# First weight piece in two parts, and the last norm's sums and updates regrouped, in a two-block kernel

## The reference

```python
def rmsnorm(x, g):
    xf = x.astype(jnp.float32)
    var = jnp.mean(xf * xf, axis=-1, keepdims=True)
    return (xf * lax.rsqrt(var + RMS_EPS) * g.astype(jnp.float32)).astype(x.dtype)
...
        h = rmsnorm(h_res, g_mix_pre[l])
        proj = h @ w_in[l]
...
        u_gate, u_val = jnp.split(u, 2, axis=-1)
        f = jax.nn.gelu(u_gate, approximate=True) * u_val
        y = f @ w_down[layer].astype(f.dtype)
        x = x + rms_norm(y, norm_ffn_post[layer])
```

## Time and profile before

| | us |
|---|---|
| median of 3 runs | 1638.5 |
| lowest and highest | 1637.44, 1638.98 |
| the profiled execution | 1639.61 |
| its span | 1637.8 |
| TensorE busy | 1594.1 (97% of the span) |
| VectorE busy | 1112.9 (68%) |
| ScalarE busy | 573.7 (35%) |
| mean granted TensorE clock | 0.991 of full |

### The profile page before, as it was taken

The page is one execution under the profiler, slowest core; times in us unless marked ns, Lnnn a source line. Parts: engine busy times, 40 slices in busy tenths (PEclk is TensorE's granted clock), DMA queues, the critical chain, the costliest instruction groups (busy, mean ns, idle before and its releaser), DMA issues.

```text
span 1637.8 us, 25145 instructions
## 1 busy us (share of the span) xinstructions
PE 1594.1 (97%) x9750; PEld 1431.9 (87%) x9750; DVE 1112.9 (68%) x1624; ACT 573.7 (35%) x826; POOL 32.7 (2%) x65
## 2 busy tenths in 40 slices
PE   8999999989999999999999999999999899999997
PEld 8999999989999988988887888877789788888887
DVE  5334556689888842288899998765557898887324
ACT  5123323442222222253334345556235322222221
POOL 1110000000000000000001101000000000000000
PEclk9999999999999999999999999999999999999999
DMA  4442212222222233233222222222221323232332
GB/s 169 115 128 90 92 63 90 65 91 89 92 90 90 90 103 103 78 110 98 95 90 85 78 84 86 87 67 89 91 91 65 100 93 102 90 102 90 103 113 81
DMA packets 45065, 152.65 MB, mean 93 GB/s; under 512 B 5978, under 2 KB 8038, under 8 KB 44992
## 3 DMA queue, kind: packets, MB, share of 16 engines
q1 hardware_dynamic: 42912, 147.26, 28.1%
q0 software_dynamic: 2080, 4.34, 1.1%
HBM read 149.44 MB, written 4.51 MB: 94 GB/s over the span
## 4 chain that ended last, share of the span: by engine, by line
PE 80%; DVE 15%; ACT 3%; issue 1%; DMA 0%; SPq 0%; DVEq 0%
PE ps L488 70%; PE ps L498 7%; DVE work L1637 6%; DVE wlo L1289 3%; DVE res L1357 1%; DVE tmp L1354 1%; ACT whi L899 1%; PE ps L782 1%; PE ps L851 1%; PE ps L704 1%; ACT probs L1160 1%; ACT L1217 0%; DVE xl L1327 0%; DVE peaks L1681 0%; PE ps L743 0%
## 5 line engine op out<-in xcount | busy, mean ns | idle before, releaser
L488 PE MATMUL ps<-xh,whi 128*128 128x258 f32 (+2 forms) x1944 | 548.2, 331 | 17.6 <-DVE wlo L1289 12.3
L488 PE MATMUL ps<-xh,wlo 128*128 128x258 f32 (+2 forms) x1944 | 541.0, 327 | 0.0
L488 PE MATMUL ps<-xl,whi 128*128 128x258 f32 (+2 forms) x1944 | 540.3, 327 | 0.0
L899 ACT ACTIVATE whi<-raw 128x1024 fp32r<-128x1024 f32 x272 | 287.1, 1057 | 452.0 <-DMA raw<-w_dram 451.6
L1289 DVE TENSOR_TENSOR wlo<-raw,whi 128x1024 fp32r<-128x1024 f32 x272 | 331.7, 1220 | 166.4 <-ACT whi L899 166.0
L488 PEld LDWEIGHTS ps<-xh,whi 128*128 128x128 f32 x1944 | 330.0, 191 | 48.7 <-issue 14.6
L488 PEld LDWEIGHTS ps<-xh,wlo 128*128 128x128 f32 x1944 | 328.6, 190 | 31.6
L488 PEld LDWEIGHTS ps<-xl,whi 128*128 128x128 f32 x1944 | 329.7, 190 | 29.3 <-issue 0.2
L1637 DVE SCALAR_TENSOR_TENSOR work<-cin,vecs,work 128x512 f32<-128x512 f32 x240 | 180.2, 751 | 6.9
L488 PE MATMUL ps<-fh,whi 128*128 128x512 f32 x264 | 103.0, 390 | 1.6 <-DVE stage L1398 0.8
L488 PE MATMUL ps<-fl,whi 128*128 128x512 f32 x264 | 102.8, 389 | 0.0
(11 more groups left out here) (228 smaller groups left out, 2072.5 us busy)
## 6 DMA issues: line engine op xcount, KB each, us to landing
raw<-w_dram SPq DMA_DIRECT2D x272, 512.0 KB, 3.5
bias_copies_dram<-bias_rows_dram POOLq DMA_DIRECT2D x12, 192.0 KB, 3.7
res<-x_dram SPq DMA_DIRECT2D x8, 264.0 KB, 6.3
out_dram<-res SPq DMA_DIRECT2D x16, 128.0 KB, 1.8
dftp<-dftp_dram POOLq DMA_DIRECT2D x1, 550.7 KB, 4.5
bias<-bias_copies_dram POOLq DMA_DIRECT2D x4, 128.0 KB, 2.5
bias<-bias_copies_dram POOLq DMA_DIRECT2D x8, 64.0 KB, 2.6
vecs<-vec_dram SPq DMA_DIRECT2D x1, 364.0 KB, 8.1
```

Of the source, the lines that this page charges most:

```text
L488: last = pe.matmul(ps[:, bank, 0:b - a], w[:, slot, cols], xx[:, k, a:b], start=start and n == 0, stop=stop and n == 2)
L899: act.activation(whi[:, slot, :], raw[:, slot, :], ACT.Copy).then_inc(w_hi, 1)
```

## The change

1. The first piece of weights is loaded in two transfers, columns 0 to 255 (128 KB, the weights of k = 0 and 1 of the first tile) before x's tile 1 and columns 256 to 1023 (384 KB) after it. ScalarE and VectorE split each part by itself. TensorE waits for `first_split` before k = 0 of the first tile and for the whole piece before its k = 2. (The wait on `tile_read` that is removed there concerned a phase with T0 = 0, where it was never made.)
2. In the last norm, at step 21 of the second half, TensorE sums `acc` (which by then holds the squares of tiles 0 to 6) over the channels into one column of PSUM banks 0 and 1 and leaves the sum open; after the last product it adds the squares of tile 7 from `sq` itself. ScalarE's root reads the two columns. VectorE's `add_half` of tile 7 is gone.
3. The last products `down` are made for two k at a time, four instructions of 2 x 256 columns, with the factor broadcast over the two.

```diff
--- before.py
+++ after.py
@@ -144,6 +144,7 @@
 SLOTS_W = 4
+FIRST = 2 * P
@@ -273,6 +274,9 @@
 
         x_landed = [sem(f"x_landed{k}") for k in range(KD)]
         gain_landed = sem("gain_landed")
+        first_landed = sem("first_landed")
+        first_hi = sem("first_hi")
+        first_split = sem("first_split")
         vec_landed = sem("vec_landed")
         onehot_landed = sem("onehot_landed")
         dft_landed = sem("dft_landed")
@@ -388,7 +392,11 @@
             sp.dma_start(vecs[:, 0:KD], vec_in[:, 0:KD]).then_inc(gain_landed, 16)
             for k in range(KD):
                 sp.dma_start(res[:, k, :], x_in[:, k, :]).then_inc(x_landed[k], 16)
-                if k % 2 == 0:
+                if k == 0:
+                    sp.dma_start(raw[:, 0, 0:FIRST], w_in[0][:, 0:FIRST]).then_inc(first_landed, 16)
+                elif k == 1:
+                    sp.dma_start(raw[:, 0, FIRST:], w_in[0][:, FIRST:]).then_inc(w_landed[0], 16)
+                elif k % 2 == 0:
                     sp.dma_start(raw[:, k // 2, :], w_in[k // 2]).then_inc(w_landed[k // 2], 16)
             sp.dma_start(vecs[:, KD:], vec_in[:, KD:]).then_inc(vec_landed, 16)
             with sp.Fori(1, CHUNKS // SLOTS_W) as it:
@@ -524,10 +532,10 @@
                         k = step - lag
                         if not 0 <= k < KD:
                             continue
-                        if k == 0:
+                        if p == 0 and k == 0:
+                            pe.wait_ge(first_split, 1)
+                        if k == (0 if p else FIRST // P):
                             pe.wait_ge(w_split, C0[phase] + p + 1)
-                            if T0[phase]:
-                                pe.wait_ge(tile_read, T0[phase])
                         if p == 0:
                             pe.wait_ge(operand_ready, ready + k + 1)
                         last = three_passes(pairs[p], p, k, k, operand, spans, k == 0, k == KD - 1)
@@ -554,6 +562,8 @@
                                 sum_channels(norm, 0)
                             if h == 1 and at == 7:
                                 spread_inverse(norm, 0)
+                            if norm == "post2f" and h == 1 and at == 21:
+                                first_sums(norm)
                             last = half_passes(banks[h][t], 0, n % 4, k, k0 + k, operand, spans[h],
                                                first and k == 0, final and k == kts - 1)
                             at += 1
@@ -693,6 +703,24 @@
                                      ones[:, 0:1], start=True, stop=True)
                 last.then_inc(sums_ready, 1)
 
+            def first_sums(name):
+
+                w, blocks = NORMS[name]
+                pe.wait_ge(sq_used, 2 + SQ[name] + KD + 1)
+                for b in range(blocks):
+                    pe.matmul(ps[0:w, b, SUMS_AT:SUMS_AT + 1], acc[:, (blocks + b) * w:(blocks + b + 1) * w],
+                              ones[:, 0:1], start=True, stop=False)
+
+            def last_sums(name):
+
+                w, blocks = NORMS[name]
+                n = SQ[name] + KD + 1
+                pe.wait_ge(sq_ready, n + 1)
+                for b in range(blocks):
+                    last = pe.matmul(ps[0:w, b, SUMS_AT:SUMS_AT + 1], sq[:, n % 2, b * w:(b + 1) * w],
+                                     ones[:, 0:1], start=False, stop=True)
+                last.then_inc(sums_ready, 1)
+
             def spread_inverse(name, h=None):
 
                 w, blocks = NORMS[name]
@@ -886,7 +914,7 @@
             one_piece_tiles("pw", KD, (sh, sl), row2, READY["silu"] - KD)
             out_tiles("out2", "post2", (xh2, xl2), row2, half2, READY["mixed"] - KD)
             ffn("up2", "down2", (xh2, xl2), row2, half2, "h2f", "f2", "post2", "pre2f", "post2f")
-            sum_channels("post2f", 1)
+            last_sums("post2f")
             spread_inverse("post2f", 1)
 
 
@@ -960,7 +988,13 @@
                 for k in range(KD):
                     act.wait_ge(x_landed[k], 16)
                     act.activation(xh[:, k, :], res[:, k, :], ACT.Identity, scale=vec("g_mix_pre", k)).then_inc(x_hi, 1)
-                    if k % 2 == 0:
+                    if k == 0:
+                        act.wait_ge(first_landed, 16)
+                        act.activation(whi[:, 0, 0:FIRST], raw[:, 0, 0:FIRST], ACT.Copy).then_inc(first_hi, 1)
+                    elif k == 1:
+                        act.wait_ge(w_landed[0], 16)
+                        act.activation(whi[:, 0, FIRST:], raw[:, 0, FIRST:], ACT.Copy).then_inc(w_hi, 1)
+                    elif k % 2 == 0:
                         w_to_hi("u", 0, k // 2)
                 squares_of_res("pre1", "u", 0, L1)
                 after_squares("pre1", "u", None)
@@ -1258,7 +1292,9 @@
             root("post2f", 0)
             second_down_half("down2", 0)
             second_down_half("down2", 1)
-            root("post2f", 1)
+            act.wait_ge(sums_ready, NTH["post2f", 1])
+            act.activation(roots[:, 0, 0:2], ps[:, 0:2, SUMS_AT], ACT.Sqrt, bias=small[:, 2:3], scale=1.0 / D) \
+               .then_inc(root_ready, 1)
 
 
         @block.vector
@@ -1476,7 +1512,15 @@
             for k in range(KD):
                 dve.wait_ge(x_landed[k], 16)
                 cut_lo(k + 1, k, "g_mix_pre", 0, L1, xh[:, k, :], xl[:, k, :])
-                if k % 2 == 0:
+                if k == 0:
+                    dve.wait_ge(first_hi, 1)
+                    dve.tensor_tensor(wlo[:, 0, 0:FIRST], raw[:, 0, 0:FIRST], whi[:, 0, 0:FIRST].bitcast(F32),
+                                      ALU.subtract).then_inc(first_split, 1)
+                elif k == 1:
+                    dve.wait_ge(w_hi, 1)
+                    dve.tensor_tensor(wlo[:, 0, FIRST:], raw[:, 0, FIRST:], whi[:, 0, FIRST:].bitcast(F32),
+                                      ALU.subtract).then_inc(w_split, 1)
+                elif k % 2 == 0:
                     w_to_lo("u", 0, k // 2)
             inverse_of_res("u", "pre1", L1)
             dve.wait_ge(vec_landed, 16)
@@ -1830,14 +1874,13 @@
             dve.wait_ge(spread_ready, NTH["post2f", 0])
             for k in range(KD):
                 updated("post2f", k, 0, down, N_META)
-                if k == 5:
-                    add_half("post2f", 1, 1)
             inverse("post2f", 1)
             dve.wait_ge(spread_ready, NTH["post2f", 1])
             c0 = SEQ // 2
-            for k in range(KD):
-                dve.tensor_tensor(down[:, k, c0:SEQ], down[:, k, c0:SEQ], stat("post2f", 1), ALU.mult) \
-                   .then_inc(update_ready, 1)
+            for k in range(0, KD, 2):
+                dve.tensor_tensor(down[:, k:k + 2, c0:SEQ], down[:, k:k + 2, c0:SEQ],
+                                  stat("post2f", 1).rearrange("p (o n) -> p o n", o=1).broadcast_to([P, 2, SEQ // 2]),
+                                  ALU.mult).then_inc(update_ready, 2)
             for k in range(TAIL_POOL, KD):
                 dve.wait_ge(update_ready, k + 1)
                 cols = res[:, k, N_META + c0:L1]
```

## The result

The changed kernel takes 1641.05 us (median of 22 runs, 1638.29 to 1646.23), the kernel before in the same comparison 1638.51 (22 runs, 1637.21 to 1640.04). The ratio is 1.0016, with a 95% interval of 1.001 to 1.0023. The ratio lies within the 0.2% that the prediction called no change, but the interval excludes 1: the changed kernel is 2.5 us slower, where 1637.2 was forecast in a range of 1635.8 to 1639.4. The profiled execution took 1640.26 us with a span of 1638.4 and a mean granted clock of 0.993.

The account below looks back on a forecast made before the run. TensorE was taken as the bound (80% of the chain), with time won only where it stands still or after its last product. Start -0.9 and end -0.37 gave -1.27: 1637.2 us against the median 1638.5, range 1635.8 to 1639.4.

Parts of the forecast that it names:

- signs of being wrong: Clock rising later than before, second piece split after 11.9, or GpSimd's third addition taking over a microsecond.
- The first split: At the start: first part of the weights split between 6.12 and 6.60, first product near 6.2, 1.6 us earlier.
- The landings: At the start: rest of the first piece lands by 6.65; the second piece's landing at 9.03 stays, its bytes ahead unchanged.
- 0.5 us won, whatever the first transfer did within its bounds: At the start: the second tile's products begin at 11.45 in place of 11.94.
- the pause before k = 2: In the first tile: TensorE waits 0.45 us, from about 9.0, for `xl` at 9.42.
- Nothing downstream takes it back: After the start: the gain stays, since TensorE does not pause again before the norm's sums.
- The clock: TensorE's rise to its upper level: at 13.4 wins nothing more, at 11.7 wins 0.8 us more; middle -0.9 for the start.
- The end: After the last product and in the stream before it: shorter norm and paired `down` products, -0.37 us in all.
- The ports shared by VectorE and GpSimd: In the last additions: if the ports exclude, VectorE starts at 1632.95 and the end is worth -0.30.
- The split changes nothing: Rival at the start: both transfers land late or the second piece slips half a microsecond; 1638.1 us, chance 0.2.
- The pauses keep the clock down: Rival at the start: new TensorE pauses delay the clock's rise to near 16.9; whole +0.9, 1639.4 us, chance 0.2.
- collide the other way: Rival at the end: VectorE's additions shut out GpSimd's third and delay the stores, +1.7; 1639.3 us, chance 0.05.

Follow-up runs that it names:

- one_transfer: Kernel before with the first piece still one transfer, but split in two parts on ScalarE and VectorE, TensorE starting on the first part; 1638.86 us, ratio 1.0002.
- warm_before: Kernel before with 16 additional products of ones by ones on TensorE ahead of its first wait, results never read; 1638.30 us, ratio 0.9998.
- end_only: Changed kernel with the start of the kernel before, so only the last norm's sums and the paired updates are new; 1638.64 us, ratio 0.9999.
- warm_after: Changed kernel with 16 additional products of ones by ones on TensorE ahead of its first wait; 1641.13 us, ratio 1.0021 against the kernel before.
- after_filled: Changed kernel with products of ones by ones put into TensorE's three pauses of the start; 1640.47 us, ratio 1.0015 against the kernel before.
- halves: Changed kernel with the first piece divided into 512 and 512 columns in place of 256 and 768; 1641.18 us, ratio 1.0012 against the kernel before.
- before_again: The kernel before, unchanged, run once more for a second profile; 1636.61 us.

## Why the prediction was wrong

The sign was wrong: -1.27 us forecast, +2.5 measured. Two of the prediction's own signs of being wrong came true: the clock rose later than before, and the second piece was split after 11.9 (at 12.42). Point by point:

- **The first split.** Forecast: first product at 6.2. Measured 6.07, 6.38, 6.10 and 6.12 in four profiles. Right, but the kernel before starts at 7.84 only in the profile that was worked from; in the three others it is 8.21, 8.21 and 8.48.
- **The landings: the step that failed.** The prediction said that the rest lands "at the latest where x's second tile landed before, 6.65", and of the second piece that its landing "is a matter of the bytes ahead of it, which don't change". Measured: about 8.2 and 10.10, so 1.5 and 1.1 us later; for the second piece 1.0 on the mean of four profiles each. The bytes ahead didn't change, but the rate did: 436 KB in place of 661 between 4 and 6 us. Why the rate fell is open. The Trainium skill (DMA: Bandwidth & Descriptors, section "Rules for kernel authors") advises to coalesce small transfers, under 64 KB above all; here the parts have 128 and 384 KB, so that row doesn't speak of them, and dividing the piece cost all the same.
- **"0.5 us won, whatever the first transfer did within its bounds"** fell with it. The second tile starts 0.52 us later in the first profiles and 0.25 on the mean of four each, not 0.49 earlier. I had 0.45 us for the pause before k = 2 and it is 1.21; the second, 0.6 by the forecast, is gone, because the first has pushed everything behind it. "Nothing downstream takes it back" failed too, as `one_transfer` and `warm_before` show at 360 to 372 us.
- **The clock.** I took the middle between a rise at 13.4 and one at 11.7, and it came at 13.9, 15.1, 15.0 and 14.4 in four profiles (13.4, 13.5, 13.7 and 12.8 in those of the kernel before). Its price was right where it was worked out and wrong for the kernel: warming TensorE up brings the rise forward by 9 us, `warm_before` is 1.0 us ahead at 23 us (I had 0.8), and the timed runs show nothing of it.
- **The end.** In the stream +0.45, as forecast. From the last product to `down` -0.88 (forecast -0.97); GpSimd 0.29 later against `down` (0.27). SP's last four stores take 1.96 us where I carried over 1.86, which had one shorter step of 0.37 among its four, another 0.1. Net -0.15 in place of -0.37: the mechanism right, three small terms each too good. `end_only` can't tell it from nothing.
- **The ports shared by VectorE and GpSimd.** VectorE's five additions took 2.09 us where they took 1.76, while GpSimd's third ran until 1633.78. Two of them took 1.08, so the 0.33 lies in the first. That is the rule cited ahead (the Trainium skill, SBUF — State Buffer, "SBUF: two separate sides"), and the trace agrees: the first addition ended 0.28 us after GpSimd's third, in all four profiles. It cost nothing, since SP's issues set the end.
- **The rivals.** None was right alone. "The split changes nothing" had the second piece slip by half a microsecond behind rows of 1 and 3 KB, at 0.2, and priced it at 0 instead of a loss. "The pauses keep the clock down" had the late rise, but its fillers and its warm-up don't bring the time back. GpSimd and VectorE did not collide the other way.
- **The range** failed at its upper end by 1.65 us: I had bounded the landings by the bytes alone and left no case in which both landings slip. The half of 1.5 us for the medians was also given to the lower end only; with it above, 1641.05 would still lie outside.

**What is shown and what is open.** Shown: a first piece divided (six edits and the changed kernel) or moved behind x's second tile costs 1.6 to 3.2 us, one in place costs nothing (four edits), and neither the clock at the start nor the division of the work is the cause. The later landing of the second piece and the fewer bytes by 9 us are in all twelve such profiles and in none of the eight others. The later second tile is not: it starts at 12.05 to 14.73 in the twelve, at 11.43 to 12.58 in the eight.

Open is the way from the landings to the 2.5 us. The four profiles of the changed kernel are 0.8 us behind at 23 us on the mean. But `warm_after`, `after_filled` and `halves` reach that place at 21.98 to 22.45, ahead of the kernel before (22.73 on the mean), and their medians are 1.7 to 3.1 us slower, while the 1.0 us that `one_transfer` and `warm_before` have there wins nothing. The profiled executions of the first three were fast ones, so their typical start may be later; no profile shows it. A part may lie in the clock far behind the start: the mean granted clock listed for each timed execution averages 0.9923 over 88 with a divided piece and 0.9929 over 101 of the kernel before. Those 0.0006 are worth 1 us at most, by an estimate from the span. They are not the whole: at a listed clock of 0.993 the 29 divided executions still average 1640.98 and the 60 of the kernel before 1638.19. A single profile can't settle this. `before_again` gains 3 us on the first profile of the same kernel between 1051 and 1178 us (granted clock 1.00 against 0.97), more than the effect.

## What to carry to other kernels

Read a prefetch at the start as one queue: before you divide a transfer or put something between, ask which later landing has the least to spare, and follow that one. Here it was the second piece, with 0.6 us. A first product that starts earlier is worth nothing while a later input decides. And time a change in the first 12 us over many runs: its effect on one profile is changed by stretches hundreds of us later, and a lag that grows between profiles from different chips need not be the change's.

## What was not expected of the hardware

- The 16 DMA engines moved less with the same bytes queued: 1.94 MB by 9 us with 128 + 384 KB in place of 512, 2.22 without. Why is open. Between 4 and 6 us the engines' busy share fell from 0.99 and 0.98 to 0.85 and 0.71, and they moved less in their busy time as well, 280 KB a us in place of 335.
- A 4 KB write to DRAM kept GpSimd waiting 2.5 or over 4 us, in executions of the same kernel: 2.5 to 2.8 us in three of four profiles from one chip, 3.8 to 4.5 in all that are known to come from the three others.
- An early rise of the clock (4.1 us in place of 13.4) left the time where it was.
